# One block for a hybrid decoder step, x tiles ahead of weights, a norm on VectorE and its scaling on ScalarE

## What is computed

```python
rq, rk, rv, rg, fq, fk, fv, ff, ga, gb = split(x @ w_in)      # 1032 x 1024 by 1024 x 6664
logf = log_sigmoid(ff + b_f)                                    # the forget gate, 8 heads
fox  = softmax(fq fk^T / 8 + cumsum(logf)_q - cumsum(logf)_k) @ fv      # 8 heads of 64
ret, state = retention in chunks of 128 (rotated rq, rk; rv; decays)    # 4 heads, 128 x 256
mix  = (sigmoid(ga) * ((silu(rg) * group_norm(ret)) @ w_pa) + sigmoid(gb) * (fox @ w_pb)) @ w_o
h    = layer_norm(2**0.25 * x + mix, ln1_w, ln1_b)
a    = gelu(causal conv of width 3 over rows of (h @ w_up)) * (h @ w_gate)     # 2816 wide
y    = layer_norm(2**0.25 * h + a @ w_down, ln2_w, ln2_b)
```

## Time and profile before

| | us |
|---|---|
| median of 3 runs | 2096.11 (2094.16 to 2099.72) |
| the profiled execution | 2099.52 |
| its span | 2097.8 |
| TensorE busy | 1969.2 |
| VectorE busy | 1144.9 |
| ScalarE busy | 652.7 |
| POOL busy | 224.8 |

### The profile page before, as it was taken

The page is one execution under the profiler, slowest core; times in us unless marked ns, Lnnn a source line. Parts: engine busy times, 40 slices in busy tenths (PEclk is TensorE's granted clock), DMA queues, the critical chain, the costliest instruction groups (busy, mean ns, idle before and its releaser), DMA issues.

```text
span 2097.8 us, 38511 instructions
## 1 busy us (share of the span) xinstructions
PE 1969.2 (94%) x14335; PEld 1841.5 (88%) x14335; DVE 1144.9 (55%) x1747; ACT 652.7 (31%) x1211; POOL 224.8 (11%) x254
## 2 busy tenths in 40 slices
PE   7899998799999999989899998899999999999996
PEld 5787897798888888878799996899999999999996
DVE  3555454877867876885433846633322333233348
ACT  4454444134133223313411303632211322123234
POOL 0000000020020020020000100500000000100005
PEclk8999999999999999999999999999999999999999
DMA  3211201787988888886832411111111111111154
GB/s 121 72 32 31 61 21 47 242 308 252 314 273 289 270 273 293 275 309 236 283 109 92 122 50 31 31 41 50 50 40 50 40 49 44 48 50 40 38 161 134
DMA packets 151698, 276.50 MB, mean 132 GB/s; under 512 B 19057, under 2 KB 57966, under 8 KB 151558
## 3 DMA queue, kind: packets, MB, share of 16 engines
q1 hardware_dynamic: 115954, 175.22, 25.1%
q0 software_dynamic: 23264, 82.83, 13.0%
q10 hardware_dynamic: 12368, 16.88, 2.2%
HBM read 247.24 MB, written 27.72 MB: 131 GB/s over the span
## 4 chain that ended last, share of the span: by engine, by line
PE 45%; DVE 3%; ACT 1%; DMA 1%; issue 0%; SPq 0%; ACTq 0%; DVEq 0%
PE bank L121 42%; PE bank L1706 2%; DVE w_lo L2061 1%; DMA gated_raw<-gated_t_scratch 1%; DVE y L2037 0%; DVE ln_stats L2046 0%; DVE z L1957 0%; DVE x_lo L1974 0%; PE bank L1646 0%; ACT z L1770 0%; PE bank L1667 0%; ACT gate L1761 0%; ACT moving_hi L1718 0%; ACT x_hi L1772 0%; PE banks L1667 0%
## 5 line engine op out<-in xcount | busy, mean ns | idle before, releaser
L121 PE MATMUL bank<-x_hi,w_hi 128*128 128x344 f32 (+1 forms) x1896 | 617.7, 326 | 35.7 <-DVE rot_sin L1299 14.4
L121 PE MATMUL bank<-x_lo,w_hi 128*128 128x344 f32 (+1 forms) x1896 | 608.5, 321 | 0.0
L121 PE MATMUL bank<-x_hi,w_lo 128*128 128x344 f32 (+1 forms) x1896 | 608.4, 321 | 0.0
L121 PEld LDWEIGHTS bank<-x_hi,w_hi 128*128 128x128 f32 (+1 forms) x1896 | 356.5, 188 | 52.1 <-issue 32.6
L121 PEld LDWEIGHTS bank<-x_hi,w_lo 128*128 128x128 f32 (+1 forms) x1896 | 356.5, 188 | 1.8 <-issue 0.3
L121 PEld LDWEIGHTS bank<-x_lo,w_hi 128*128 128x128 f32 (+1 forms) x1896 | 356.5, 188 | 1.7 <-issue 0.2
L97 ACT ACTIVATE w_hi<-w_raw 128x1024 fp32r<-128x1024 f32 (+3 forms) x139 | 141.8, 1020 | 407.4 <-PE bank L121 366.2
L121 PE MATMUL bank<-moving_lo,w_hi 128*128 128x344 f32 x744 | 237.5, 319 | 0.0
L121 PE MATMUL bank<-moving_hi,w_hi 128*128 128x344 f32 x744 | 225.3, 325 | 4.8 <-DVE moving_hi L1868 2.5
L104 DVE TENSOR_TENSOR w_lo<-w_raw,w_hi 128x1024 fp32r<-128x1024 f32 (+3 forms) x139 | 164.4, 1182 | 96.3 <-ACT w_hi L97 95.0
L121 PE MATMUL bank<-moving_hi,w_lo 128*128 128x344 f32 x648 | 208.1, 321 | 0.0
(11 more groups left out here) (297 smaller groups left out, 2855.7 us busy)
## 6 DMA issues: line engine op xcount, KB each, us to landing
cache_keys<-in_cache_k_dram SPq DMA_DIRECT2D x256, 256.0 KB, 4.8
cache_vals<-in_cache_v_dram SPq DMA_DIRECT2D x256, 256.0 KB, 5.2
w_raw<-in_w_in_dram POOLq DMA_DIRECT2D x52, 512.0 KB, 6.2
w_raw<-in_w_up_dram POOLq DMA_DIRECT2D x22, 512.0 KB, 4.5
w_raw<-in_w_gate_dram POOLq DMA_DIRECT2D x22, 512.0 KB, 4.5
tail_raw<-in_w_down_dram SPq DMA_DIRECT2D x22, 448.0 KB, 3.7
gate<-gate_t_scratch SPq DMA_DIRECT2D x15, 516.0 KB, 3.5
w_raw<-in_w_down_dram POOLq DMA_DIRECT2D x10, 448.0 KB, 4.3
```

The lines of the kernel that those rows point to most:

```text
L121: mm = pe.matmul(g.bank[n][0:m, 0:TC], w[slot][:, k, 0:m], x[:, k, chunk(n)], start=(k == 0 and i == 0), stop=(k == kt - 1 and i == 2))
```

## The change

The four stages' functions no longer open a block each. They return what each engine does, and `build_program` puts the four behind each other in one block. Where the block's end had kept an order, semaphores are waited for instead. Five more edits go with it.

1. One block. ScalarE and VectorE wait at the start of `retain` for the stored attention output (`fo_stored`), ScalarE also for the stored keys and values, SP for `fo_stored` ahead of the first cache pages. SP takes over what ScalarE had waited for at the end of `retain`. TensorE's first attention product waits for `bias_out`, the copies out of its banks.
2. `prepare`: x tiles come ahead of the weights. ScalarE and VectorE split the forget gate's weight behind six x tiles and attention's first weight behind all of them; POOL loads the latter behind the two gathers of forget values.
3. The forget gate's low weight half is written into columns 32 to 39 of the same stationary. One matmul with 40 columns gives both products with `x_hi` (output rows 0 to 7 and 32 to 39), a second one with 8 columns adds `x_lo`; VectorE adds the two row groups, three times 8x344.
4. `fox`: VectorE makes the cumulative sum first, then the low half of the second weight, then the key parts.
5. First layer norm: VectorE multiplies by weight and inverse root in one operation, ScalarE adds the bias and writes `x_hi` in one pass, VectorE makes `x_lo` from z, bias and `x_hi`. `z` is left without the bias, and `acc` = 2**0.25 z + 2**0.25 bias is written by ScalarE, one tile of 1032 columns in each of the first eight up and gate tiles; POOL does none of it. The centring of all three chunks stands ahead of the weight's low half.
6. Tiles: the second tile's up product waits only until the first up product has been copied out, and its weight is split ahead of the first tile's convolution.

The diff without the changed indentation, cut:

```diff
-def product(g, pe, jb, xh, xl, kt=KD, m=P, before=None, ready=None, after=None):
+def product(g, pe, jb, xh, xl, kt=KD, m=P, before=None, ready=None, after=None, freed=None):
-        pe.wait_ge(g.bank_free[n], j + 1)
+        pe.wait_ge(g.bank_free[n], j + 1 if freed is None else freed)
...
 # prepare, TensorE
-    product(g, pe, job(0, 0, 0), g.xh, g.xl, m=FH)
+    for n in range(NCH):
+        pe.wait_ge(g.bank_free[n], 1)
+        for k in range(KD):
+            pe.matmul(bank[n][0:FF_M, 0:TC], g.w_hi[0][:, k, 0:FF_M], g.xh[:, k, chunk(n)], start=(k == 0), stop=False,
+                      skip_group_check=True)
+            mm = pe.matmul(bank[n][0:FH, 0:TC], g.w_hi[0][:, k, 0:FH], g.xl[:, k, chunk(n)], start=False, stop=(k == KD - 1),
+                           skip_group_check=True)
+        mm.then_inc(g.mm_chunk, 1)
 # prepare, ScalarE
-    split_hi(g, act, job(0, 0, 0), KD, FH)
-    split_hi(g, act, job(0, 0, 1))
-    with act.Fori(0, QB // STAGES) as it:
-        for u in range(STAGES):
-            round_half(it * STAGES + u, u, P, g.xh[:, :, ds((it * STAGES + u) * P, P)])
+    for q in range(QB):
+        if q == FF_AT:
+            split_hi(g, act, job(0, 0, 0), KD, FF_M)
+        round_half(q, q % STAGES, P, g.xh[:, :, q * P:(q + 1) * P])
     round_half(QB, 0, NS, g.xh[:, :, SEQ:T])
+    split_hi(g, act, job(0, 0, 1))
 # prepare, VectorE
+    for n in range(NCH):
+        dve.wait_ge(ff_act, n + 1)
+        dve.tensor_tensor(z[:, chunk(n)], z[:, chunk(n)], bank[n][LO_AT:FF_M, 0:TC], ALU.add).then_inc(g.bank_free[n], 1)
 # prepare, POOL
-    load_weight(g, pool, job(0, 0, 0), w_in_tile(a, C_FF, FH), KD, FH)
-    load_weight(g, pool, job(0, 0, 1), w_in_tile(a, C_FQ))
+    load_weight(g, pool, job(0, 0, 0), w_in_tile(a, C_FF, FF_M), KD, FF_M)
...
+    load_weight(g, pool, job(0, 0, 1), w_in_tile(a, C_FQ))
 # retain, SP
     load_q(1, 1)
+    sp.wait_ge(g.fo_stored, FH // 2 * 16)
...
-    sp.wait_ge(fos_stored, 16 * (FH // 2))
+    sp.wait_ge(turned, NS)
+    sp.wait_ge(g_stored, RH * 32)
+    for b in range(2):
+        sp.wait_ge(gate_stored[b], stored_until(b, RH - 1, 12))
+    sp.wait_ge(st_stored, RH * 16)
+    sp.wait_ge(fin_stored, RH * 16)
 # retain, ScalarE
+    act.wait_ge(g.fo_stored, FH // 2 * 16)
+    for u in range(2):
+        act.wait_ge(g.kv_stored[u], FH // 4 * 32)
     split_hi(g, act, job(J0, 1, 1))
 # finish, POOL
-    for k in range(NCH):
-        pool.wait_ge(h_full, (k + 1) * KD)
-        pool.wait_ge(h_lo, (k + 1) * KD)
-        for t in range(KD):
-            ins = pool.tensor_scalar(acc[:, t, chunk(k)], z[:, t, chunk(k)], ALPHA, None, ALU.mult)
-        ins.then_inc(h_scaled, 1)
 # finish, TensorE
+    up_and_gate_of(1, 0, ju, freed=ju + 2)
 # finish, ScalarE: h_high, then each tile of the first section
-    act.activation(z[:, k, chunk(n)], z[:, k, chunk(n)], ACT.Identity, scale=ln_cols[:, 0, k:k + 1], bias=ln_cols[:, 1, k:k + 1]).then_inc(h_full, 1)
-    act.wait_ge(h_full, n * KD + k + 1)
-    act.activation(g.xh[:, k, chunk(n)], z[:, k, chunk(n)], ACT.Copy).then_inc(h_hi, 1)
+    act.activation(g.xh[:, k, chunk(n)], z[:, k, chunk(n)], ACT.Identity, bias=ln_cols[:, 1, k:k + 1]).then_inc(h_hi, 1)
...
+    if s == 0:
+        act.activation(acc[:, ds(i, 1), :].rearrange("p a t -> p (a t)"), z[:, ds(i, 1), :].rearrange("p a t -> p (a t)"),
+                       ACT.Identity, scale=ALPHA, bias=fc[:, 20:21]).then_inc(h_scaled, 1)
 # finish, VectorE
     centre(0)
-    split_lo(g, dve, job(JF, JF % 2, 1))
     centre(1)
     centre(2)
+    split_lo(g, dve, job(JF, JF % 2, 1))
 # scale, h_low
-    dve.tensor_tensor(z[:, k, chunk(n)], z[:, k, chunk(n)], rstd[:, chunk(n)], ALU.mult).then_inc(normed, 1)
+    dve.scalar_tensor_tensor(z[:, k, chunk(n)], z[:, k, chunk(n)], ln_cols[:, 0, k:k + 1], rstd[:, chunk(n)], ALU.mult, ALU.mult).then_inc(normed, 1)
-    dve.tensor_tensor(g.xl[:, k, chunk(n)], z[:, k, chunk(n)], g.xh[:, k, chunk(n)].bitcast(F32), ALU.subtract).then_inc(h_lo, 1)
+    dve.scalar_tensor_tensor(g.xl[:, k, chunk(n)], z[:, k, chunk(n)], ln_cols[:, 1, k:k + 1], g.xh[:, k, chunk(n)].bitcast(F32), ALU.add, ALU.subtract).then_inc(h_lo, 1)
```

2900 lines of the change are left out of this document (1466 added, 1434 removed).

## The result

The changed kernel takes **2082.79 us** (median of 5 runs, 2075.31 to 2084.45) against 2096.11: a ratio of 0.9921, 95% interval 0.9904 to 0.9938. The same kernel in a second batch: 2086.01 us, ratio 0.9952 (0.9934 to 0.9970). The gain is real and some 13 us, the mean of the two ratios. I had forecast 28.6 us and a time of 2067.5, with 2078 as the upper end. The profiled execution took 2084.45 us, its span is 2082.7. One run of the kernel before, in the first batch of experiments, took 3702 us at a clock of 0.923, a slow state, and is left out everywhere.

A forecast was written before the change was run, and what follows sets the result against it. TensorE, busy for 94% of the span, was taken to bound the kernel, so gains come from its work or its waits. The terms 6.2 + 4.0 + 2.9 + 4.1 + 2.5 + 2.3 + 1.5 + 5.1 = 28.6 us gave 2067.5 us, range 2060 to 2078.

The forecast's parts named there:

- x tiles and forget gate: Start: x loaded ahead of the weights, 6.2 us, and the gate's product in fewer matmuls, 4.0 us.
- x term: Start: with x first, the last x tile lands near 19.5 us; 6.2 us gained, ends 4.3 and 8.4.
- The product's 4.0: Forget gate's product: 48 matmuls in place of 72, 4.0 us gained on the path.
- Forget gate to attention: VectorE's chain before the second attention product: 3.57 us of standing removed, an addition and a wait added; 2.9 us gained.
- Attention to first keys: Boundary from attention to retention: earlier loads let VectorE use cached keys sooner; 4.1 us gained, range 2.3 to 5.5.
- Retention to the rest: Boundary behind the retention: gated-row loads start sooner and one weight tile is gone from them; 2.5 us, ends 0.6 and 4.3.
- Layer norm: First layer norm and first feed-forward tiles: three terms, 2.3 + 1.5 + 5.1 us gained.
- (a) and (b): Layer norm: (a) VectorE's second centring no longer waits for a weight, 2.3 us; (b) POOL's 24 scalings are gone, 1.5 us.
- three signs of being wrong: Last x tile after 24 us, TensorE busy under 0.92 of the retention, or tiles 1 to 7 over 22.8 us each.
- the loads decide more: Rival: moving loads may only reorder them, so start, boundaries and retention yield less; 2075 us, chance 0.18.
- a last x tile that doesn't move: Start, case of the loads rival: shared DMA engines make load order gain nothing; 2074 us, chance 0.04.
- Slower: Rival: retention becomes bound by cache loads throughout, making the kernel 8.5 us slower, 2104.6 us; chance 0.03.

The follow-up runs named there:

- start_old: The changed kernel with the whole first stage of the kernel before (weights ahead of x, forget gate's product in 72 matmuls): 2085.99 us, ratio 0.9941.
- filled_start_old: The changed kernel with spare matmuls in TensorE's waits and gated-row loads ahead of four stores, but the first stage of the kernel before: 2074.52 us, ratio 0.9897.
- hold_product: The changed kernel, with TensorE's first product behind the retention held until SP comes to the first gated-row load: 2084.79 us, ratio 0.9944.
- rest_filled: gated_first with spare matmuls, whose results nobody reads, in TensorE's waits for the gated rows: 2080.41 us, ratio 0.9922.
- gated_first: The changed kernel, with SP issuing the first four loads of gated rows ahead of the last four stores: 2082.39 us, ratio 0.9929.
- Fillers, with the order on SP: gated_first with spare matmuls at the pairs of heads, behind the retention, ahead of w_pb and in the layer norm: 2069.89 us, ratio 0.9873.
- filled_all_old: The changed kernel with spare matmuls and gated-row loads ahead of four stores, but old start, old norm and four blocks: 2096.99 us, ratio 0.9998.
- norm_old: The changed kernel with the layer norm and first feed-forward tiles of the kernel before: 2091.47 us, ratio 0.9979.
- norm_old_tile_new: norm_old with only the change's part that concerns the second feed-forward tile: 2087.31 us, ratio 0.9960.
- fill_and_gated_first: gated_first with spare matmuls in TensorE's waits at the head of each pair of heads: 2074.45 us, ratio 0.9892.
- filled_blocks: The changed kernel with spare matmuls and gated-row loads ahead of four stores, but its four stages in four blocks: 2082.15 us, ratio 0.9931.
- fill_attention: The changed kernel with spare matmuls, whose results nobody reads, in TensorE's waits at the head of each pair of heads: 2080.53 us, ratio 0.9920.

## Why the prediction was wrong

Two terms of the sum failed, and with them its silent premise, that what a place gains reaches the end at full clock. The start's 10.2 us was priced from one execution that was slow in just this place: where neither kernel has a slow stretch in the product it is 6.1 us, and the additions take 1.5 of them back. The boundary behind the retention, 2.5 us, turned into a loss of 3: the loads did not start sooner, and TensorE's clock fell on work that now decides. Against the forecast, by place, the start lacks 4.1 us, the chain behind it 1.6, the first keys 1.1, the boundary behind the retention 5.6, the layer norm 0.5 and the retention 0.8, together 13.7 of the 15 that are missing; the attention's 0.2 to 4.4 us come on top. By place:

- **x tiles and forget gate**, 10.2: the profiles gave 10.7 and 8.5, which is luck. The last x tile landed at 21.05 us in the first profile and 21.04 in the second, inside my bounds of 17.3 and 21.4 but not at the 19.5 that I took; before it landed at 25.57 and 24.10 us. So the x term of 6.2 measures 4.5 and 3.1: it was over-sized. The product's 4.0 was right (11.5 us in `start_old`, 7.7 in the changed kernel, both at full clock). What filled the sum up to 10.7 is a slow stretch of 6.8 us that both profiles of before have just ahead of the product and in it, and in the first a last x tile 1.6 us later than in `start_old` (23.95). `start_old` has no slow stretch there and reaches the product's end at 39.0 us, 3 to 5 us ahead of both, with the same code up to there. `filled_start_old` has 39.2.
- **Forget gate to attention**, 2.9: 1.2 and 1.3. The block's 3.57 us went (0.48 stays). What I put at 0.5 us, the additions, cost 1.5: to VectorE's `logf` it is 7.80 us from the product's end, before 6.31. Two of the three additions were to lie beside the product. The rows show all three after it (33.70), because ScalarE, which copies the product's other half for them, comes to it only at 33.15: the page totals ahead of it in its order came only 2.7 us earlier (30.28, before 33.00), the product's end 10.7 us. I had looked only at the engine that was late before.
- **Attention to first keys**, 4.1: 2.9 and 3.1, inside its range of 2.3 to 5.5. From SP's first load to the key loads it is 6.86 us in both kernels. SP's start came 2.3 us earlier, as priced; from the key loads to their first use it is 6.4 us where it was 7.0, a gain of 0.6 us where the sum has 1.8.
- **Retention to the rest**, 2.5: -3.0 and -3.3, outside its range. "The loads decide" was right (`hold_product`), and that TensorE's gap turns into a wait as well (4.02 us). Wrong was that the loads start sooner: 5.65 us behind the last value product before and after, because the same stores are still ahead of them on SP. And what came in addition is the clock: a slow stretch of 13.7 us on w_pa's products, where the kernel before has full clock. Filling the waits took it away and gave 4.1 us (`rest_filled` against `gated_first`).
- **Layer norm**, 8.9: 8.6 and 8.2; split 5.2 and 4.0 against 5.1 and 3.8. Right in sum and in parts. The Trainium skill, "SBUF — State Buffer", section "Terms", would have made it 5.6 us more by its rule on the shared port pair; the traces don't bear that out, 4.0 us for (a) and (b) together, where that rule would have 9.4.
- **Not edited**, 0: the attention lost 4.4 us in one pair of profiles and 0.2 in the other, by chance of how long the clock was slow, retention 0.9 and 0.6.

None of my three signs of being wrong appeared: the last x tile landed before 24 us, TensorE was busy for 0.946 of the retention's 430 to 1000 us, and tiles 1 to 7 took 22.64 us each. None of them looked at the clock or at the boundary.

The rivals: "the loads decide more" (2075 us) had the right sign and too little of it. Its case of a last x tile that doesn't move, which is also what the rule in the prediction would give, is not what the rows show: the tile landed 4.5 and 3.1 us earlier. "Slower" did not come near: retention is as long as before. None of mine had the clock in it, though the rows of before showed the slow stretches: I read the layer norm's (1.8 us) and gave the others no line.

How much is the clock? Fillers, with the order on SP, bring the changed kernel's granted clock from a mean of 0.980 (11 runs) to 0.990 and its time down by 13.3 us, as much as the whole change had brought. In `filled_all_old` the clock is 0.986, against 0.981 in the kernel before (72 runs), and the time is the same within the interval; 3.4 us of that are the cost of VectorE's order with blocks apart, so it says little about the kernel before. Between runs of one kernel, the time follows the clock: each microsecond of full clock lost (1 minus the mean clock, times the 2080 us) costs 0.49 us (± 0.06, standard error, 72 runs) in the kernel before. In the changed kernel it is 0.94 (± 0.18, 11 runs), but in its five close relatives without fillers in one block (`start_old`, `norm_old`, `norm_old_tile_new`, `gated_first`, `hold_product`; 39 runs, each kernel about its own mean) it is 0.50 ± 0.09. So a steeper slope after the change is not shown. The Trainium skill, "TensorE: Matmul & The Clock Gate", section "Terms", puts the penalty at half of the time spent at half rate, which in these units is 1 for a kernel that TensorE bounds throughout; the measured 0.49 and 0.50 are half of that. My reading is that the waits which the change removed had covered slow stretches: TensorE was slow where something else decided. The rows show this behind the retention, where the slow stretch moved from the product ahead of the loads onto w_pa. For the kernel as a whole it is an interpretation.

**Open.** Both profiles of the kernel before were above its median (2099.5 and 2102.2 us against 2096.4 over 64 runs), so 3 to 6 us of the 15.1 and 17.0 are such executions' bad luck. The start accounts for about that much: 43.7 and 42.2 us at the end of the forget gate's product, where the three other kernels with the old start have 39.0, 39.2 and 40.1. Why the start is slow in some executions stays open; it is so in two profiles with the new start too (36.2 in `fill_and_gated_first`, 38.5 in `filled_blocks`, 32.4 to 33.7 in the others). Open is also what makes the retention 650 or 660 us long, and why `fill_attention` gained 3.5 us by its median and 5.6 or more in the attention of its profile.
